# Inverting the unit-triangular blocks of a gated DeltaNet: the other triangle by its own product instead of by a transposition, and the level masks on GpSimd

## What is computed

```
h += 1/2 * SwiGLU_1(RMSNorm(h))
u  = RMSNorm(h); P = u @ w_in        # q|k|v|z|beta|alpha of 4 DeltaNet heads x 128, and a GLU pair of 512
h += concat(DeltaNet heads, 31-tap depthwise conv channels) @ w_out
h += 1/2 * SwiGLU_2(RMSNorm(h));  final RMSNorm
```

```
a_mat = einsum(kb, k) * decay * strict
m_mat = eye + a_mat
sol   = triangular_solve(m_mat, [vb, kb * exp(gc)], unit_diagonal)
u_c, w_c = sol
v_new = u_c - w_c @ s;  o = (q * exp(gc)) @ s + att @ v_new;  s = s * exp(g_last) + k_scaled^T @ v_new
```

## Time and profile before

| | us |
|---|---|
| median of 3 runs | 1383.44 (1381.44 to 1384.04) |
| the profiled execution | 1381.44 |
| its span, first to last instruction | 1379.6 |
| busy: PE / PEld / DVE / ACT / POOL | 1267.4 / 1229.9 / 665.1 / 457.8 / 225.1 |
| mean granted TensorE clock | 0.959 |

### The profile page before, as it was taken

One profiled execution on the slowest core, in us unless ns is written; L12 is line 12 of the kernel. 1 busy time (PEld: TensorE's weight loads), 2 busy tenths in 40 slices (PEclk: granted clock), 3 DMA queues, 4 the chain that ended last, 5 costly groups with the idle time before them and its releaser, 6 DMA issues.

```text
span 1379.6 us, 22341 instructions
## 1 busy us (share of the span) xinstructions
PE 1267.4 (92%) x9041; PEld 1229.9 (89%) x9041; DVE 665.1 (48%) x822; ACT 457.8 (33%) x698; POOL 225.1 (16%) x157
## 2 busy tenths in 40 slices
PE   5999999999999999986666788998999999999995
PEld 4999999999999899985565777698999999999994
DVE  5443234432437437895667652734443344433443
ACT  5432122221224465555542322424322122212232
POOL 3000000000002266445742003130000000000011
PEclk9999999999999999997889997699999999999997
DMA  6222222222223213110000000331222222222252
GB/s 207 94 76 92 77 77 76 80 87 76 76 82 101 92 50 119 61 61 31 1 1 1 1 0 16 114 101 53 93 79 90 76 91 76 92 76 77 91 95 72
DMA packets 35830, 100.45 MB, mean 73 GB/s; under 512 B 11840, under 2 KB 12224, under 8 KB 35392
## 3 DMA queue, kind: packets, MB, share of 16 engines
q1 hardware_dynamic: 35632, 97.33, 22.2%
q10 hardware_dynamic: 144, 2.36, 0.5%
HBM read 94.24 MB, written 5.44 MB: 72 GB/s over the span
## 4 chain that ended last, share of the span: by engine, by line
PE 76%; DVE 14%; issue 4%; ACT 3%; POOL 2%; DMA 0%; POOLq 0%; DVEq 0%; ACTq 0%; SPq 0%
PE ps L372 67%; PE ps L451 8%; DVE work L1199 4%; POOL work L1497 2%; DVE work L1224 1%; DVE work L1197 1%; ACT w_hi L733 1%; DVE x_lo L1063 1%; DVE d_inv_t L1326 1%; DVE d_t L1321 1%; DMA raw<-weights 0%; PE ps L426 0%; PE ps L559 0%; DVE d_decay L1264 0%; DVE h L1451 0%
## 5 line engine op out<-in xcount | busy, mean ns | idle before, releaser
L372 PE MATMUL ps<-x_hi,w_hi 128*128 128x296 f32 (+1 forms) x1920 | 422.3, 301 | 31.8 <-DVE x_lo L1063 20.1
L372 PE MATMUL ps<-x_lo,w_hi 128*128 128x296 f32 (+1 forms) x1920 | 418.2, 299 | 0.0
L372 PE MATMUL ps<-x_hi,w_lo 128*128 128x296 f32 (+1 forms) x1920 | 417.0, 299 | 0.0
L372 PEld LDWEIGHTS ps<-x_hi,w_hi 128*128 128x128 f32 x1920 | 313.8, 191 | 36.1 <-issue 22.7
L372 PEld LDWEIGHTS ps<-x_lo,w_hi 128*128 128x128 f32 x1920 | 314.1, 190 | 0.0
L372 PEld LDWEIGHTS ps<-x_hi,w_lo 128*128 128x128 f32 x1920 | 312.5, 190 | 0.0
L1058 DVE TENSOR_TENSOR w_lo<-raw,w_hi 128x1024 fp32r<-128x1024 f32 x168 | 208.3, 1241 | 206.4 <-ACT w_hi L733 204.1
L733 ACT CAST w_hi<-raw 128x1024 fp32r<-128x1024 f32 x168 | 174.8, 1041 | 256.8 <-PE ps L372 229.0
L372 PE MATMUL ps<-g_hi,w_hi 128*128 128x296 f32 (+1 forms) x704 | 152.5, 298 | 1.0 <-DVE g_lo L1088 1.0
L372 PE MATMUL ps<-g_lo,w_hi 128*128 128x296 f32 (+1 forms) x704 | 152.0, 297 | 0.0
L372 PE MATMUL ps<-g_hi,w_lo 128*128 128x296 f32 (+1 forms) x704 | 151.4, 296 | 0.0
(11 more groups left out here) (198 smaller groups left out, 1100.7 us busy)
## 6 DMA issues: line engine op xcount, KB each, us to landing
raw<-weights SPq DMA_DIRECT2D x168, 512.0 KB, 3.3
h<-x_t SPq DMA_DIRECT2D x2, 1184.0 KB, 5.7
new_state<-S ACTq DMA_DIRECT2D x1, 2304.0 KB, 8.3
y_t<-h SPq DMA_DIRECT2D x8, 288.0 KB, 2.4
S<-states SPq DMA_DIRECT2D x1, 2048.0 KB, 10.6
mask<-masks SPq DMA_DIRECT2D x1, 836.5 KB, 7.9
c_ext<-hist_c SPq DMA_DIRECT2D x4, 120.0 KB, 8.5
last_c<-c_ext SPq DMA_DIRECT2D x4, 120.0 KB, 8.8
```

Source lines behind the costliest of these rows:

```text
L372: last = nc.tensor.matmul(ps[:, slot, half, 0:w_half], w[:, slot, k, :], x[:, k, a:a + w_half], start=(k == 0 and n == 0), stop=(k == kt - ...
```

## The change

A level has two steps now. The mask moves from the product to the matrix: GpSimd multiplies `AT` with the level's mask into a buffer `BM` ahead of the level (`blocks`, once per level; the first behind `start`, each further one behind the product that read the one before). PE multiplies `BM` with `X`, and ACT, not DVE, copies the result into `T1`. Then PE forms both `Y^T T1` (bank b) and `T1^T Y` (bank a), and DVE subtracts the first from `X` and the second from `Y`. The transposition and ACT's copy of it are gone, at the last level the product for `X` too. A chain of tiles 0 to 3 has 15 steps where it had 20, that of tile 4 has 9 where it had 11; the numbers 10 and 4 at which the schedule cuts the chains are as they were. The masks are stored in the other orientation.

```diff
-    chain = [[("start", t, i) for i in range(2)] + [("level", t, 3 * l + i) for l in range(1, LEVELS[t]) for i in range(3 if l < LEVELS[t] - 1 else 2)]
+    chain = [[("start", t, i) for i in range(2)] + [("level", t, 2 * l + i) for l in range(1, LEVELS[t]) for i in range(2)]
              + [("end", t, 0)] for t in range(NT)]
@@ tensor @@
             def level(t, i):
                 if i == 0:
+                    pe.wait_ge(s["b_ready"][p], lx + l)
                     pe.wait_ge(s["x_inv"][p], lx + l)
                     pe.wait_ge(s["y_ready"][p], ly + l)
                     for hd in range(H):
-                        last = mm(heads(a, n)[0:n, hd, :], AT[p][0:n, hd, 0:n], X_[p][0:n, hd, 0:n])
+                        last = mm(heads(a, n)[0:n, hd, :], BM[p][0:n, hd, 0:n], X_[p][0:n, hd, 0:n])
                     last.then_inc(s["t1_ps"][p], 1)
-                elif i == 1:
+                else:
                     pe.wait_ge(s["t1_ready"][p], lx + l)
+                    for hd in range(H if l < LEVELS[t] - 1 else 0):
+                        mm(heads(b, n)[0:n, hd, :], Y_[p][0:n, hd, 0:n], T1[p][0:n, hd, 0:n])
                     for hd in range(H):
                         last = mm(heads(a, n)[0:n, hd, :], T1[p][0:n, hd, 0:n], Y_[p][0:n, hd, 0:n])
                     last.then_inc(s["p_ps"][p], 1)
-                else:
-                    pe.wait_ge(s["y_ready"][p], ly + l + 1)
-                    for hd in range(H):
-                        last = nc.tensor.transpose(bank(b)[0:n, hd * P:hd * P + n], Y_[p][0:n, hd, 0:n], m("ident", n))
-                    last.then_inc(s["xt_ps"][p], 1)
@@ scalar @@
             def level(t, i):
-                if i == 2:
-                    act.wait_ge(s["xt_ps"][p], lx - LXO[t] + l)
-                    nc.scalar.copy(X_[p][0:n, :, 0:n], heads(b, n)[0:n]).then_inc(s["x_inv"][p], 1)
+                if i == 0:
+                    act.wait_ge(s["t1_ps"][p], lx + l)
+                    nc.scalar.copy(T1[p][0:n, :, 0:n], heads(a, n)[0:n]).then_inc(s["t1_ready"][p], 1)
@@ vector @@
             def level(t, i):
-                if i == 0:
-                    dve.wait_ge(s["t1_ps"][p], lx + l)
-                    V.tensor_tensor(T1[p][0:n, :, 0:n], heads(a, n)[0:n], over_heads(m("levels", n, l), n),
-                                    ALU.mult).then_inc(s["t1_ready"][p], 1)
                 if i == 1:
                     dve.wait_ge(s["p_ps"][p], lx + l)
+                    dve.wait_ge(s["x_inv"][p], lx + l)
+                    if l < LEVELS[t] - 1:
+                        V.tensor_tensor(X_[p][0:n, :, 0:n], X_[p][0:n, :, 0:n], heads(b, n)[0:n],
+                                        ALU.subtract).then_inc(s["x_inv"][p], 1)
                     dve.wait_ge(s["y_ready"][p], ly + l)
                     V.tensor_tensor(Y_[p][0:n, :, 0:n], Y_[p][0:n, :, 0:n], heads(a, n)[0:n],
                                     ALU.subtract).then_inc(s["y_ready"][p], 1)
@@ gpsimd @@
+            def blocks(t, l):
+                n = TILES[t][1]
+                p = t % 2
+                G.tensor_tensor(BM[p][0:n, :, 0:n], AT[p][0:n, :, 0:n], over_heads(m("levels", n, l), n),
+                                ALU.mult).then_inc(s["b_ready"][p], 1)
             def start(t, i):
-                pass
+                if i == 0:
+                    pool.wait_ge(s["at_ready"], t + 1)
+                    blocks(t, 1)
             def level(t, i):
-                pass
+                l, i = i // 2, i % 2
+                p, a, b, ly, lx = chain_at(t)
+                if i == 1 and l + 1 < LEVELS[t]:
+                    pool.wait_ge(s["t1_ps"][p], lx + l)
+                    blocks(t, l + 1)
```

More of the change, by code:

```diff
@@ L77 @@
 LVO = [0, 0, 7, 7, 14]
-LXO = [0, 0, 1, 1, 2]
 def merge(a, b):
@@ L154, in shape_masks @@
         a = MASK["levels"].start + l * P
-        above = (s // (2 * w) == c // (2 * w)) & (s % (2 * w) < w) & (c % (2 * w) >= w)
-        m[:, a:a + P] = above.T if l else above
+        m[:, a:a + P] = (s // (2 * w) == c // (2 * w)) & (s % (2 * w) < w) & (c % (2 * w) >= w)
     m[:, MASK["group"]] = seq[:, None] == np.arange(NG)[None, :]
@@ L205, in ring @@
             return [sb(f"d_{name}{i}", [P, H, P], F32, zone) for i in range(n)]
-        G_B, B_B, E_, ES, AT, _, X_, T1 = [ring(n, 2) for n in ("g_b", "beta_b", "decay", "decay_strict", "a_t", "rest", "inv",
-                                                                 "t1")]
+        G_B, B_B, E_, ES, AT, BM, X_, T1 = [ring(n, 2) for n in ("g_b", "beta_b", "decay", "decay_strict", "a_t", "b",
+                                                                  "inv", "t1")]
         Y_ = ring("inv_t", 2)
@@ L300, in build @@
         s = {n: sem(n) for n in names}
-        for n in ("y_ready", "x_inv", "xt_ps", "t1_ps", "t1_ready", "p_ps"):
+        for n in ("b_ready", "y_ready", "x_inv", "t1_ps", "t1_ready", "p_ps"):
             s[n] = [sem(f"{n}{i}") for i in range(2)]
@@ L540, in level @@
             def level(t, i):
-                l, i = i // 3, i % 3
+                l, i = i // 2, i % 2
                 n = TILES[t][1]
```

3 lines of the change are left out of this document (2 added, 1 removed).

## The result

The changed kernel takes 1390.69 us (median of 5, 1388.62 to 1391.94) where the kernel before takes 1382.38 (median of 5, 1381.44 to 1384.04): ratio 1.0056, 95% interval 1.0042 to 1.0072. It is slower, by 8.3 us; forecast was 6 us faster. The profiled execution took 1390.11 us.

A forecast was written before the change was run, and what follows sets the result against it. It took the stages as bound by results passing between engines through in-order lists, no engine being full. 0 - 15.4 + 3 + 1 + 2 + 3 = -6.4 us, so 1377.0 us as median; 8-in-10 range 1366 to 1391.

The forecast's parts named there:

- The schedule: Chain cut after ten steps: one level visit fewer in stage 2 (8.4 us) and in stage 4 (7.0), together -15.4 us.
- Take-back: Stages 1 and 3 lengthen from levels moved there, with more VectorE subtractions and taps: +3 us, ends -3 and +11.
- second product: PE's extra product in 22 levels, mostly hidden where PE has time free: +1 us, ends 0 and +8.
- Late masks: GpSimd's masks: first one 2.7 us late at level 1, later ones just covered: +2 us, ends 0 and +14.
- The rival's mechanism: Levels wait for GpSimd because masks end after their level's Y, delaying both chains: 1394 us, chance 0.25.
- GpSimd against DVE: DVE's taps held up beside GpSimd's masks in the stages, half of 6.1 us on the path: +3, ends 0 and +25.
- taps of DVE far above 1.2 us each the lock: Sign in DVE's taps: times far above 1.2 us each would show the port lock between VectorE and GpSimd.
- PE waiting for GpSimd: Sign in the list of waits: would show GpSimd had become what the levels wait for, forecast 1394 us, chance 0.25.
- Wrong if stages 1 and 3 grow by more than 2 and 4 shrink: Stated test over the four stages of the chains: such growth would make the prediction wrong.
- The rule of the Trainium skill: VectorE and GpSimd share SBUF ports exclusively; each of 27 masks could stop two-SBUF-input taps once, up to +25 us.

The follow-up runs named there:

- e2: The changed kernel without the masks, TensorE reading the unmasked AT, so the level masks are left out of what is computed: 1371.69 us, ratio 0.9924.
- e15: Kernel before with second product and X's subtraction replacing the transposition, VectorE keeping masks, chains cut after 14 of 20 steps, taps' sum in PSUM: 1387.31 us.
- e4: Kernel before with the second product and X's subtraction in place of the transposition and ScalarE's copy, masks still on VectorE: 1405.58 us, ratio 1.0151.
- e8: Kernel before with one number changed, chains 1 and 3 cut after 14 of their 20 steps: 1378.14 us, ratio 0.9974.
- e3: Changed kernel with an empty third step in each level but the last, so chains are cut as before: 1392.77 us, ratio 1.0075.
- e5: Changed kernel with each GpSimd mask over only 2 of 128 columns, waits kept, TensorE reading unmasked AT (level masks not computed): 1371.66 us, ratio 0.9929.
- e9: Changed kernel with VectorE's running sum of the convolution taps in PSUM for the first 24 taps, masks kept: 1373.36 us, ratio 0.9935.
- e17: Changed kernel without the masks (level masks left out of what is computed) and with the taps' running sum in PSUM: 1364.99 us, ratio 0.9882.

## Why the prediction was wrong

- **The schedule, -15.4:** 12.2 in the changed kernel. Stage 2 gave 10.1 for 8.4; part of that difference is my reading of the last Y of tile 1, 1.5 us too early, which makes the pace 8.9 a level and not 8.4. Stage 4 gave 2.1 for 7.0: up to the last Y of tile 3 it gave 5.9, but the scan's path goes on through tile 4, whose first level came 4.5 us behind it. That what follows waits for the last Y of tile 3 was the mistake here. Without masks (e2) the two stages gave 11.2 and 3.8.
- **Take-back, +3, and second product, +1:** e2, which has both, lost 2.5 in stage 1 and 2.5 in stage 3. Right in sum. By themselves the parts can't be priced so: on a VectorE that keeps the masks the second product cost 14.5 to 23 (e15, e4), outside my 0 to +8, and the later cut alone took back 16.6 (e8), outside my -3 to +11.
- **Everything but GpSimd:** -15.4 + 3 + 1 is -11.4; e2 measured -10.5. In part this is luck. The schedule with what it takes back, -12.4 in my sum, is worth 3.8 us in the kernel before (e8) and 2.1 in the changed one (e3); most of e2's gain must come with what DVE's single visit to a level gives back, which I had put at nothing. The changed order without masks and without the later cut was not run, so the parts of the 10.5 stay open.
- **Late masks, +2:** 0 (e5 equals e2; with masks of full length e9 has stages 1 and 2 as long as e17). The rival's mechanism, masks that end after their level's Y, did not occur; its 1394 was near the measured time by another cause.
- **GpSimd against DVE, +3: this is the step that failed.** It measured 19.0 (changed over e2). The bound of 25 held it, the value taken did not. My scaling from the share of GpSimd's work gave 6.1 us of held-up taps; they were 8.3 (51.3 against 43.0), so this part was nearly right. Two others were wrong. I looked at the taps alone, where VectorE has 15.0 us more: the rest are mainly first-level Ys (4.6 to 6.5 for four, 0.5 to 2.2 for the small one) and copies. And I took half of it to be hidden beside VectorE's idle time, where nothing was hidden: 15.0 us of VectorE came with 19.0 of time.
- **The signs I had named:** "taps of DVE far above 1.2 us each the lock": a tap, two instructions, is 1.7 us. "PE waiting for GpSimd": not seen. "Wrong if stages 1 and 3 grow by more than 2 and 4 shrink": 19.7 against 12.2.

The rule of the Trainium skill cited in the prediction put the term near its upper end, and I set it aside for the average of the stages. As a warning it was the better guide; its nearness in number is luck, since the 25 was counted in taps, of which 8.3 us came true. That the lock works in the other direction too is seen weakly: two masks beside the taps take 2.99 us (706.30) and 2.52 with the taps' sum in PSUM (704.93 in e9), but on average a mask takes 1414 ns in the one kernel and 1387 in the other.

## What to carry to other kernels

Before work is moved to GpSimd, list VectorE's instructions with two SBUF inputs, and its SBUF-to-SBUF copies, that the same event releases: beside a mask of 1.3 us each was held up by 0.9 to 1.1 us here (0.69 to 1.63, 0.42 to 1.49), and this counted in full where results pass between engines in lists worked off in order. Look first whether such an accumulation can stand in PSUM, which here was worth 6.7 us without any other change. When an engine waits often and for short times in such a chain, don't take its idle time for cover: price each microsecond added to it at one, and take the price as a first guess, since the pairs above lie between 0.7 and 1.7.
